# A two-layer decoder trunk on one core: x loaded in four quarters, one block ahead, and the squares of a layer norm summed on GpSimd

## What is computed

```python
def conformer_conv(a, b, dw, dw_b, ln_g, ln_b, w_conv_out):
    u = a * jax.nn.sigmoid(b)
    u = lax.conv_general_dilated(u, dw[:, None, :], ...) + dw_b   # causal, 31 taps, each channel by itself
    u = jax.nn.silu(layer_norm(u, ln_g, ln_b))                    # over 512 channels
    return u @ w_conv_out

def hybrid_mixer(h, w_in, ...):
    a, b, p, gc, gp = jnp.split(h @ w_in, IN_SPLITS, axis=-1)
    yc = conformer_conv(a, b, ...)
    yp = multiscale_pool(p, w_pool, pool_scale)
    return (jax.nn.sigmoid(gc) * yc + jax.nn.sigmoid(gp) * yp) @ w_out

for layer in range(2):
    x = x + hybrid_mixer(rms_norm(x, mix_norm[layer]), ...)
    h = rms_norm(x, ffn_norm[layer])
    x = x + (swiglu(h, ...) if layer == 0 else moe_ffn(h, ...))   # layer 1: 2 of 8 experts
return rms_norm(x, final_norm)
```

## Time and profile before

| | |
|---|---|
| median of 3 runs | 1419.75 us (1419.68 to 1420.81) |
| the profiled execution, its own time | 1420.94 us |
| its span, first to last instruction | 1419.2 us |
| busy: TensorE / VectorE / ScalarE / GpSimd | 1405.4 / 1176.6 / 985.3 / 212.8 us |
| mean granted TensorE clock | 0.997 |

### The profile page before, as it was taken

How to read it: one execution, slowest core, us unless ns; L and a number is a source line. 1 busy time by engine, 2 the same in 40 slices (tenths; PEclk the granted TensorE clock), 3 DMA queues, 4 the chain that set the end, 5 groups by cost and what they waited for, 6 DMA issues and landing times.

```text
span 1419.2 us, 18324 instructions
## 1 busy us (share of the span) xinstructions
PE 1405.4 (99%) x6490; PEld 1166.0 (82%) x6490; DVE 1176.6 (83%) x1069; ACT 985.3 (69%) x869; POOL 212.8 (15%) x251
## 2 busy tenths in 40 slices
PE   9999999999999999999999999999999999999997
PEld 7888888888888888888888888888888888888885
DVE  6997544548987998889899898888989889888896
ACT  7765434347765877867867777786786777778675
POOL 6840000005831101001001001000100100100020
PEclk9999999999999999999999999999999999999998
DMA  9656555545548899999999999999999999999992
GB/s 360 213 177 216 181 180 193 191 152 204 171 170 303 287 402 363 370 369 410 375 383 371 390 369 371 388 384 356 409 373 383 370 390 370 368 396 389 363 389 85
DMA packets 197840, 446.45 MB, mean 315 GB/s; under 512 B 8570, under 2 KB 20138, under 8 KB 197792
## 3 DMA queue, kind: packets, MB, share of 16 engines
q1 hardware_dynamic: 192496, 432.57, 80.8%
q0 software_dynamic: 2592, 8.87, 2.3%
q10 hardware_dynamic: 2704, 4.38, 0.9%
HBM read 438.49 MB, written 7.86 MB: 315 GB/s over the span
## 4 chain that ended last, share of the span: by engine, by line
PE 93%; DVE 4%; DMA 1%; ACT 1%; SPq 0%; issue 0%; POOL 0%; ACTq 0%; POOLq 0%
PE bank L1482 29%; PE bank L1484 29%; PE bank L1483 29%; PE bank L1662 2%; DVE bank L1057 2%; DVE w_lo L1008 2%; DMA raw<-in_w_in_dram 1%; PE bank L1540 1%; ACT w_hi L674 1%; PE bank L1829 0%; DMA out_dram<-tokA 0%; SPq L460 0%; PE bank L1624 0%; PE bank L1804 0%; PE bank L1618 0%
## 5 line engine op out<-in xcount | busy, mean ns | idle before, releaser
L1008 DVE TENSOR_TENSOR w_lo<-raw,w_hi 128x2048 fp32r<-128x2048 f32 x256 | 582.8, 2291 | 134.3 <-ACT w_hi L674 134.1
L674 ACT ACTIVATE w_hi<-raw 128x2048 fp32r<-128x2048 f32 x256 | 488.1, 1912 | 200.1 <-PE bank L1484 198.8
L1482 PE MATMUL bank<-w_hi,dT_hi 128*128 128x512 f32 (+1 forms) x756 | 296.3, 392 | 0.0
L1484 PE MATMUL bank<-w_hi,dT_lo 128*128 128x512 f32 (+1 forms) x756 | 293.2, 388 | 0.0
L1483 PE MATMUL bank<-w_lo,dT_hi 128*128 128x512 f32 (+1 forms) x756 | 292.6, 387 | 0.0
L1482 PE MATMUL bank<-w_hi,cT_hi 128*128 128x512 f32 x492 | 194.3, 395 | 0.0
L1484 PE MATMUL bank<-w_hi,cT_lo 128*128 128x512 f32 x492 | 191.7, 390 | 0.0
L1483 PE MATMUL bank<-w_lo,cT_hi 128*128 128x512 f32 x492 | 191.6, 389 | 0.0
L1484 PEld LDWEIGHTS bank<-w_hi,dT_lo 128*128 128x128 f32 x756 | 141.9, 188 | 29.4
L1482 PE MATMUL bank<-w_hi,hT_hi 128*128 128x512 f32 x416 | 164.1, 394 | 1.3 <-DVE hT_lo L1022 1.0
L1482 PEld LDWEIGHTS bank<-w_hi,dT_hi 128*128 128x128 f32 x756 | 142.0, 188 | 28.4
(11 more groups left out here) (260 smaller groups left out, 1859.0 us busy)
## 6 DMA issues: line engine op xcount, KB each, us to landing
raw<-in_moe_w_gate_dram SPq DMA_DIRECT2D x96, 1024.0 KB, 7.5
raw<-in_moe_w_up_dram SPq DMA_DIRECT2D x72, 1024.0 KB, 10.3
raw<-in_moe_w_down_dram SPq DMA_DIRECT2D x72, 1024.0 KB, 9.0
raw<-in_w_in_dram SPq DMA_DIRECT2D x20, 1024.0 KB, 5.7
mix<-in_moe_w_up_dram SPq DMA_DIRECT2D x16, 1024.0 KB, 8.5
gates<-in_moe_w_down_dram SPq DMA_DIRECT2D x16, 1024.0 KB, 11.2
gates<-in_moe_w_up_dram SPq DMA_DIRECT2D x16, 1024.0 KB, 8.7
work<-in_moe_w_down_dram SPq DMA_DIRECT2D x16, 1024.0 KB, 10.9
```

The lines of the kernel that those rows point to most:

```text
L674: act.activation(w_hi[split_place(u, seen.item is not None)][:, 0:width], place[slot][:, 0:width], ACT.Copy).then_inc(hi_ready, 1)
L1008: dve.tensor_tensor(w_lo[split][:, 0:width], place[slot][:, 0:width], w_hi[split][:, 0:width].bitcast(F32), ALU.subtract).then_inc(lo_read ...
L1482: nc.tensor.matmul(dst, a_hi, b_hi, start=start, stop=False)
L1484: return nc.tensor.matmul(dst, a_lo, b_hi, start=False, stop=stop)
```

## The change

1. x comes in four quarters of 256 KB, each ahead of the two weight pieces that it belongs to; the small vectors other than the first gain are loaded by SP, behind the eight pieces and ahead of unit 2.
2. TensorE turns one quarter in front and the next after blocks 0, 1 and 3; the small vectors after block 6. Fillers in front: 5 and 4, in place of 5, 3 and 2.
3. ScalarE and VectorE treat block, piece, block, piece for k = 0 and 1, then piece and block. The first sum of squares stands after block 5.
4. In layer 0, VectorE does `u_rows(1)` before the low part of unit 5 and not after it, with four taps more ahead of it.
5. `SHARED` is 14: in each layer one tap goes from VectorE to ScalarE and GpSimd.
6. GpSimd adds the squares of groups 0 and 1, and of 2 and 3; the mean of squares takes two matmuls. GpSimd does this ahead of the first gate scaling.
7. The last read of `sums` is issued from GpSimd, not SP.

```diff
-    SHARED = 13
+    SHARED = 14
...
-            for n in range(FIRST):
-                load_x(n)
-                load_pieces(n, STREAM[n])
+            for q in range(4):
+                load_x(q)
+                load_piece(2 * q)
+                load_piece(2 * q + 1)
+            row = 0
+            for v, per in ((ffn_norm, KD), (conv_dw_b, CC), (conv_ln_g, CC), (conv_ln_b, CC)):
+                sp.dma_start(late_rows[row:row + L * per, :], v.rearrange("l (k p) -> (l k) p", p=P)).then_inc(late_landed, 16)
+                row += L * per
...
-            sp.wait_ge(scattered, n_items * 16)
-            for b in range(TB):
-                sp.dma_start(xs[:, b, :], sums[b * P:(b + 1) * P, :]).then_inc(sums_landed, 16)
...
+                for i in range(2):
+                    pool.wait_ge(centred_sq, seen.next(centred_sq))
+                    pair_of = sq[:, 2 * i * S:(2 * i + 1) * S]
+                    pool.tensor_tensor(pair_of, pair_of, sq[:, (2 * i + 1) * S:(2 * i + 2) * S], ALU.add).then_inc(sq_paired, 1)
+
                 pool.wait_ge(gain_landed, seen.next(gain_landed, 16))
...
+            for b in range(TB):
+                pool.dma_start(xs[:, b, :], sums[b * P:(b + 1) * P, :]).then_inc(sums_landed, 16)
...
+                act.wait_ge(vecs_ready, 1)
+                for k in range(2):
+                    block(k)
+                    piece(k)
+                for k in range(2, KD):
+                    piece(k)
+                    block(k)
+                    if k == 5:
+                        act.wait_ge(x_landed[3], 16)
                         sum_of_squares(0)
...
-                conv_taps(8)
-                split_to(U + 6)
-                u_rows(1, M.high)
+                if l:
+                    conv_taps(8)
+                    split_to(U + 6)
+                    u_rows(1, M.high)
+                else:
+                    conv_taps(12)
+                    u_rows(1, M.high)
+                    split_to(U + 6)
...
-                    if k == 1:
-                        transpose_loaded(1)
-                    if k == 5:
+                    if k in (0, 1, 3):
+                        transpose_loaded((k + 3) // 2)
+                    if k == 6:
                         turn_vectors()
...
-                    for c in range(CC):
-                        if c % 2 == 0:
-                            pe.wait_ge(centred_sq, seen.next(centred_sq))
-                        last = nc.tensor.matmul(bank[M.var][:, 0:S], mean_w[:, :], sq[:, c * S:(c + 1) * S], start=c == 0, stop=c == CC - 1)
+                    for c in (0, 2):
+                        pe.wait_ge(sq_paired, seen.next(sq_paired))
+                        last = nc.tensor.matmul(bank[M.var][:, 0:S], mean_w[:, :], sq[:, c * S:(c + 1) * S], start=c == 0, stop=c == 2)
...
-            idle_products(3)
             transpose_loaded(0)
-            idle_products(2)
+            idle_products(4)
```

More of the change, by code:

```diff
@@ L1101, in first_input, with block, piece @@
                 dve.wait_ge(vecs_ready, 1)
-                for k in range(KD):
+                def block(k):
+                    dve.wait_ge(hT_hi_ready, seen.next(hT_hi_ready))
+                    operand_block(k, hT_of, hT_rest, V_MIX, spread_blocks)
+                def piece(k):
                     part = slice((k % PIECES) * N, (k % PIECES + 1) * N)
```

53 lines of the change are left out of this document (26 added, 27 removed).

## The result

| | before | changed |
|---|---|---|
| median of 6 runs each, us | 1419.78 | 1429.10 |
| lowest and highest run, us | 1419.29, 1421.50 | 1425.77, 1432.20 |
| ratio of the runs, 95% interval | | 1.0064 (1.0048 to 1.0081) |
| profiled execution: time, span, us | 1420.94, 1419.2 | 1427.90, 1426.0 |

Slower by 9.3 us by the medians, 0.66%. The direction was forecast, the size was not: 1424.2 us was predicted, and 1429.1 lies above the range's end of 1426.6. The runs spread over 6.4 us where those of before spread over 2.2. Each run comes with its mean granted TensorE clock, and the order is nearly the same: 0.998 for 1425.77 us, 0.996 for the profiled 1427.90, 0.997 for 1428.06, 0.994 for 1430.13, 0.992 for 1431.42 and 1432.20.

What follows compares the result with a forecast made beforehand. TensorE, busy 1405.4 of 1419.2 us, was taken to bound the kernel. Front and layer 0 -1.4, adds of squares +4.4, clock +1.5 gave +4.5 us: 1419.75 to 1424.2 us, range 1419.5 to 1426.6.

Steps and rivals of the forecast that it cites:

- Unit 2: Front, end of the first slab: unit 2 lands by 15.9 us, 0.8 us earlier; bounds 0.3 later to 1.3 earlier.
- the later issue leaves next to no hole: Unit 2's DMA, issued at some 10.3 us instead of 6.35, still lands earlier because full bandwidth bounds it.
- Rival 3: Front: unit 2, issued 4 us later, lands no earlier; 0.4 to 0.6 of 1.4 us left, 1423.6 to 1425; chance 0.08.
- The tap given away: Layer 0's mean: one tap fewer shortens VectorE's chain by 0.4 us; GpSimd takes 0.88 us more.
- just in time: GpSimd, with the extra tap's add, still delivers its sum in time for the mean in both layers.
- Layer 0 up to the mean and the front: Start to layer 0's mean: -1.4 us from unit 2 0.8, the tap 0.4, meeting GpSimd 0.2; bounds -0.3 to -1.9.
- The rest: 0: Moved read of `sums`, used only by the last norm, costs 0; fillers cost nothing if they end before 6.95 us.
- The adds of squares: Both layers' statistics: adds held up by VectorE's low parts cost +2.2 us per layer, +4.4 us; bounds -1.1 and +5.0.
- Rival 2: Statistics: GpSimd's adds pass beside VectorE's low parts, -0.5 us per layer, 1417.3 us; chance 0.12.
- The clock: Behind the statistics: TensorE's gap brings one clock fall in the two layers, +1.5 us (0 to +3.5); chance 0.3.
- The neighbour with a fall in both layers: Behind the statistics: TensorE's clock falls in both layers, 1425.8 us; chance 0.2.
- The rival that the clock holds: Behind the statistics: no fall of the clock, the same sum without +1.5, 1422.8 us; chance 0.25.

Runs made afterwards that it cites:

- e2: Kernel before with the adds of squares on GpSimd as the only edit: 1427.65 us, +7.0 us against before.
- e5: Kernel before with `u_rows(1)` ahead of the low part as the only edit, 13 shared taps: 1419.13 us, -0.8 us against before.
- e6: Kernel before with `u_rows(1)` ahead of the low part and 14 shared taps: 1419.27 us, -0.7 us against before.
- e1: Changed kernel with the mean of squares as before (four matmuls, no GpSimd adds): 1421.63 us against 1420.62 before, +1.0 us.
- e4: Changed kernel with idle TensorE products ahead of the two matmuls of squares, filling its waits: 1426.22 us, +5.6 us against before.
- e3: Changed kernel with VectorE's low parts in the statistics held until GpSimd has added both pairs of squares: +9.5 us against before.
- e7: Kernel before with the changed front alone; 13 taps, u's rows and squares as before: +2.0 us against before.
- e9: e7 with the six small vector DMAs on SP's queue behind unit 2 instead of ahead of it: +0.6 us against before.
- e14: e9 with six more tiny activations, each with a wait, at the start of ScalarE's program: -0.5 us against before.
- e18: e1 with six more activations in ScalarE's program: +0.4 us against before.

## Why the prediction was wrong in its size

- **First product**: 6.95 forecast, 7.07 measured.
- **Unit 2**: the step "the later issue leaves next to no hole" failed. It lands 1.1 us later, not 0.8 earlier (0.3 to 1.1 over the seven profiles with that order); with the six small DMAs behind it, it lands at 15.7 to 16.7. I had counted the issue (10.3 forecast, 9.95 measured) and then let the bandwidth overrule it. Rival 3 was this case, with 0.08.
- **The waits that the front was to shorten** came from one profiled execution that lay 1.19 us above its median. In the profiles of e2, e5 and e6, which have the same front, unit 2 lands at 16.4 to 16.6 and TensorE does not wait for it. So part of the 0.8 us was probably not there to be won in a median run.
- **u's rows**: the turning without a wait, as forecast, and 0.8 us by e5. **The tap given away**: "just in time" was 0.4 us late; it gains nothing of the 0.4, loses 0.3 at the mean and makes GpSimd the last.
- **Layer 0 up to the mean and the front**, -1.4 forecast, +1.0 measured by e1. Of these 2.4 us, some 0.5 are **ScalarE's stand ahead of the last norm**, which no term held. "The rest: 0" looked at where the moved instructions arrive, and not at the program that they leave.
- **The adds of squares**: this term was right, +4.4 forecast, +4.6 measured (e4 less e1). The 0.60 us behind a low part and 2.15 us behind an add, read from the earlier trace rows, held to 0.05 us. Rival 2 fell with the changed kernel's first add, which ended 0.58 us behind the low part; e3 adds that they do take 0.7 us each when VectorE makes no low part. The Trainium skill (SBUF — State Buffer, section on who interferes with whom) says that an instruction of VectorE with two inputs in SBUF and one of GpSimd that reads SBUF exclude each other for a whole instruction. The traces agree: here a 2.3 us low part does that to a 0.73 us add, and in e3 the gate scaling to the low parts.
- **The clock**: +1.5 forecast, +3.7 measured (2.9 to 4.9 by the pair of medians that is taken). The price of one stretch was near (1.7 us measured), their number was not: the step "one fall in the two layers" failed. The median run has the time of two to three, and one run in six, by its time and its clock of 0.998, had none. The neighbour with a fall in both layers, 1425.8 with a chance of 0.2, was nearer, and 3.3 us too low, of which the front's term is 2.4. The rival that the clock holds describes at most the lowest run. The rule that I had cited from the Trainium skill (TensorE: Matmul & The Clock Gate, section on the HAM oscillation) would have left all of these 3.7 us out; here idle times of 0.5 and 2.0 us, with 0.7 us of work between them, sufficed in most executions, and 1.95 us in the profiled one of e7.

Sum of the terms as measured: +1.0 + 4.6 + 3.7 = 9.3, against -1.4 + 4.4 + 1.5. That these add up is no test, since they are differences along one row of kernels (before, e1, e4, changed). What they show is where the 4.8 us lie by which the forecast was low: 2.4 in the front with layer 0, 0.2 in the adds, 2.2 in the clock.

## What to carry to other kernels

Before work is given to an idle engine on a path that another waits for, look at what that engine shares with its neighbour at that moment: two adds of 0.73 us among low parts cost 2.5 us of waiting per layer, to save two matmuls of 0.4, and with the low parts moved out of their way the kernel was just as slow. Count a wait of TensorE of about 2 us not by its length alone but with the clock behind it, which here added more than half to the bill and spread the runs; idle products in the wait take that part away. And a DMA moved to another queue has three places to be priced: what stands behind it there (unit 2), what it had left, and the program of the engine that no longer issues it.

## What the hardware did that was not expected

- A wait of 2.0 us of TensorE, 0.7 us of work after one of 0.5, brings the granted clock to 1.2 GHz in some executions and not in others, at the same place: behind layer 1 in the changed kernel's profiles, behind layer 0 in e2's. In the changed kernel TensorE was at work again for 1.3 us before the fall.
- Six small DMAs (4 to 62 KB, 144 KB in all) ahead of a unit of 1 MB on SP's queue delay its landing: 17.0 to 17.8 us in seven profiles, against 15.7 to 16.7 in six with the unit first. The six issues themselves take 2.3 us.
- ScalarE's stand behind its last loop was 0.8 to 3.1 us over twenty profiles of kernels whose instructions there are the same, at three levels that its own program ahead of it sets; six instructions at its start moved it by 0.7 us (e9 to e14) to 2.3 us (e1 to e18).
